# Per-head sums of a delta-rule layer, taken transposed and spread back by a sixteen-row product

## The reference, cut to what matters

```
xs_j = x + mu_j * (x_before - x)                # six mixes of a token and the one before it
r, k, v = xs_0 W_r, xs_1 W_k, xs_2 W_v          # three 1024x1024 products
decay, a = two low-rank products (rank 64) of xs_3, xs_4
g  = sigmoid(xs_5 G1) G2                        # the gate, a low-rank product (rank 128)
kk = k * k_k / max(|k * k_k| over a head, 1e-12)    # sum "kk"
bonus = (sum over a head of r * k * r_k) * v        # sum "bonus"
y  = delta rule(r, decay, k, v, kk, a)
y  = (y - mean over a head) / sqrt(variance over a head + 64e-5)   # sums "mean", "var"
out = ((y * gn_g + bonus + gn_b) * g) W_o
```

## Time and profile before

| | us |
|---|---|
| median of 3 runs | 2188.06 (2187.59 to 2189.05) |
| the profiled execution, its own time | 2188.55 |
| its span, first to last instruction | 2186.7 |
| TensorE busy | 2125.8 (97%) |
| VectorE busy | 1523.9 (70%) |
| ScalarE busy | 1171.2 (54%) |
| GpSimd busy | 380.8 (17%) |
| mean granted TensorE clock | 0.994 of full speed |

### The profile page before, as it was taken

One profiled execution on the slowest core, in us unless ns is written; L12 is line 12 of the kernel. 1 busy time (PEld: TensorE's weight loads), 2 busy tenths in 40 slices (PEclk: granted clock), 3 DMA queues, 4 the chain that ended last, 5 costly groups with the idle time before them and its releaser, 6 DMA issues.

```text
span 2186.7 us, 40730 instructions
## 1 busy us (share of the span) xinstructions
PE 2125.8 (97%) x16760; PEld 1912.0 (87%) x16760; DVE 1523.9 (70%) x2118; ACT 1171.2 (54%) x2038; POOL 380.8 (17%) x357
## 2 busy tenths in 40 slices
PE   8999999999999999999999999999999988999998
PEld 5888989888888889889888998988889978898887
DVE  6797757688769877676876686477567544647754
ACT  4564456565546644675655575465447532446542
POOL 0141022111102110221111003120142540123001
PEclk9999999999999999999999999999999999999999
DMA  7987772467768877625666555355543400434552
GB/s 303 356 301 271 263 251 98 164 238 265 247 235 294 295 251 275 228 88 174 214 219 205 185 173 177 111 176 183 192 147 123 154 4 3 144 122 164 186 188 98
DMA packets 116680, 424.61 MB, mean 194 GB/s; under 512 B 12944, under 2 KB 14736, under 8 KB 115600
## 3 DMA queue, kind: packets, MB, share of 16 engines
q1 hardware_dynamic: 112896, 409.52, 53.6%
q10 hardware_dynamic: 3600, 12.49, 1.5%
HBM read 418.29 MB, written 3.67 MB: 193 GB/s over the span
## 4 chain that ended last, share of the span: by engine, by line
PE 84%; DVE 6%; issue 4%; ACT 4%; POOL 1%; DMA 1%; SPq 0%; DVEq 0%; ACTq 0%; POOLq 0%
PE banks L598 82%; DVE weight_lower L1715 2%; POOL heap L3018 1%; PE banks L1132 1%; ACT weight_upper L2444 1%; DMA weight_ring<-w_ada_row_dram 0%; PE banks L1535 0%; DVE heap L2209 0%; ACT xn_t L2622 0%; DVE xn_t L1936 0%; DMA weight_ring<-w_in_dram 0%; DVE heap L2055 0%; DVE xn_t L1933 0%; ACT heap L2655 0%; DVE silu L1930 0%
## 5 line engine op out<-in xcount | busy, mean ns | idle before, releaser
L1715 DVE TENSOR_TENSOR weight_lower<-weight_ring,weight_upper 128x1024 fp32r<-128x1024 f32 x580 | 742.2, 1287 | 278.0 <-ACT weight_upper L2444 276.5
L598 PE MATMUL banks<-xn_halves,weight_upper 128*128 128x512 f32 (+1 forms) x3680 | 809.6, 342 | 0.8 <-DVE xn_halves L2038 0.7
L2444 ACT ACTIVATE weight_upper<-weight_ring 128x1024 fp32r<-128x1024 f32 x580 | 607.9, 1054 | 283.6 <-PE banks L598 189.7
L598 PEld LDWEIGHTS banks<-xn_halves,weight_upper 128*128 128x128 f32 x3680 | 619.2, 190 | 63.5 <-issue 1.1
L598 PE MATMUL banks<-xn_halves,weight_lower 128*128 128x256 f32 x2832 | 525.9, 284 | 4.5 <-DVE xn_halves L1748 2.1
L598 PEld LDWEIGHTS banks<-xn_halves,weight_lower 128*128 128x128 f32 x2832 | 436.7, 191 | 29.1 <-DVE xn_halves L1748 3.2
L598 PE MATMUL banks<-hidden,weight_upper 128*128 128x512 f32 x1216 | 312.0, 395 | 0.6 <-DVE heap L2180 0.6
L3018 POOL TENSOR_TENSOR heap<-heap 128x256 f32<-128x256 f32 x120 | 121.9, 1020 | 884.9 <-ACT heap L2741 590.5
L598 PEld LDWEIGHTS banks<-hidden,weight_upper 128*128 128x128 f32 x1216 | 215.6, 188 | 40.0 <-DVE heap L2180 0.7
L1726 DVE CUSTOM_DVE_ANT_0 weight_ring<-weight_ring,c_rows,vecs 128x1024 f32<-128x1024 f32 x140 | 185.8, 1331 | 20.9 <-DMA weight_ring<-w_ada_dram 20.4
L598 PEld LDWEIGHTS banks<-hidden,weight_lower 128*128 128x128 f32 x1216 | 166.7, 188 | 16.2
(11 more groups left out here) (312 smaller groups left out, 2402.8 us busy)
## 6 DMA issues: line engine op xcount, KB each, us to landing
weight_ring<-w_ada_dram SPq DMA_DIRECT2D x140, 512.0 KB, 4.6
weight_ring<-ffn_gate_dram SPq DMA_DIRECT2D x88, 512.0 KB, 3.8
weight_ring<-ffn_up_dram SPq DMA_DIRECT2D x88, 512.0 KB, 4.5
weight_ring<-ffn_down_dram SPq DMA_DIRECT2D x88, 512.0 KB, 3.4
weight_ring<-m_w_up_dram SPq DMA_DIRECT2D x64, 512.0 KB, 3.2
weight_ring<-m_w_down_dram SPq DMA_DIRECT2D x64, 512.0 KB, 3.2
weight_ring<-w_in_dram SPq DMA_DIRECT2D x58, 512.0 KB, 3.9
weight_ring<-b_w_rkv_dram SPq DMA_DIRECT2D x24, 512.0 KB, 3.8
```

The costliest lines, as they stand in the source:

```text
L598: return nc.tensor.matmul(o, w, r, start=first, stop=last)
L1715: V.tensor_tensor(w_lo[:, n % RING, :], ring[:, n % RING, :], w_hi[:, j % SPLITS, :].bitcast(F32), ALU.subtract).then_inc(*did("weight_low ...
L2444: A.activation(w_hi[:, j % SPLITS, :], ring[:, n % RING, :], ACT.Copy).then_inc(*did("weight_upper", j))
```

## The change

Four things change, all in this layer.

1. **Head sums transposed.** `head_of` becomes a 128x32 matrix of zeros with two columns of ones in it. For block k a window of 16 columns is taken from it, so that the ones stand in columns 2k and 2k+1; it is the stationary operand, and the data, 128x256, is the moving one. Eight products accumulate into 16 partitions of bank 6: heads on partitions, tokens along the row.
2. **Spread by a sixteen-row product.** A new constant `of_head`, 16 rows by 1024 columns, has a one where a head owns a channel. Block k is the product of its 16x128 piece (stationary) with the 16x256 numbers (moving). The four `widen` copies go, and the steps between sum and spread work on 16x256 numbers instead of 128x32.
3. **Gate input by one VectorE operation.** `xs_5` is made like `xs_0` to `xs_2`; ScalarE's eight parts go, and VectorE makes the eight blocks of `xs_5` in one go after those of `xs_0`.
4. **The gate's low-rank product later.** `lora_in(5)` moves behind item 2 of the r projection, and ScalarE's sigmoid with it.

`head_of` and `of_head` lie in `delta_consts`, which grows from 128x832 to 128x1888 numbers in one transfer; TensorE waits for it before `head_sums("kk")`.

```diff
-    c["head_of"] = np.kron(np.eye(2), np.ones((RN, 1)))
+    at = np.arange(2 * RH)[None, :]
+    c["head_of"] = at == RH - 1 + np.arange(P)[:, None] // RN
+    c["of_head"] = np.zeros((P, D))
+    c["of_head"][0:RH] = np.kron(np.eye(RH), np.ones((1, RN)))
...
-        wide = {n: slots(i, QT * RH * RN) for n, i in (("kk", 5), ("bonus", 11), ("mean", 4), ("var", 5))}
+        per_head = {n: slots(i, S)[0:RH, :] for n, i in (("kk", 5), ("bonus", 11), ("mean", 4), ("var", 5))}
...
-                    for t in range(QT):
-                        mn = mm(bank[:, 6, t * RH + 2 * k:t * RH + 2 * k + 2],
-                                src[:, k, t * P:(t + 1) * P], const("head_of"), True, True)
+                    a = RH - 1 - 2 * k
+                    mn = mm(bank[0:RH, 6, 0:S], const("head_of")[:, a:a + RH], src[:, k, :], k == 0, k == KD - 1)
...
-                    for t in range(QT):
-                        c = t * RH + 2 * k
-                        mn = mm(cols(b, P, (k % 2) * S + t * P), wide[name][:, c * RN:(c + 2) * RN], ident,
-                                True, True)
+                    mn = mm(cols(b, S, (k % 2) * S), const("of_head", RH)[:, k * P:(k + 1) * P], per_head[name],
+                            True, True)
...
-                lora_in(5, P)
+                pe.wait_ge(*of("delta_consts_in", 0))
                 head_sums("kk", kk_sq, "kk_sq")
...
                     if f in (1, 3):
                         lora_pair(2 * f - 2)
+                    if f == 2:
+                        lora_in(5, P)
...
-                shifted_halves(0, 5)
+                shifted_halves(0)
+                for k in range(KD):
+                    dve.wait_ge(*due("xs_lower", (1, k)))
+                    shifted(5, k)
                 dve.wait_ge(*due("rkv_raw", (1, KD - 1)))
                 shifted_halves(2)
...
-                step(V.tensor_scalar(stat[:, 0, :], stat[:, 0, :], 1e-12, None, ALU.max))
-                step(V.reciprocal(stat[:, 0, :], stat[:, 0, :]))
-                widen("kk", 0)
+                step(V.tensor_scalar(kk, kk, 1e-12, None, ALU.max))
+                step(V.reciprocal(kk, kk), [("head_stat", "kk")])
...
-                    act.wait_ge(*due("xs_lower", (1, f)))
-                    part(5, f)
                     xs_upper(0, f)
                 for k in range(KD):
                     xs_upper(2, k)
                 act.wait_ge(*due("head_sums", "kk"))
-                A.activation(stat[:, 0, :], bank[:, 6, 0:QT * RH], ACT.Sqrt).then_inc(
+                A.activation(per_head["kk"], bank[0:RH, 6, 0:S], ACT.Sqrt).then_inc(
-                lora(5, P, ACT.Sigmoid)
...
                     if f in (1, 3):
                         lora_pair(2 * f - 2)
+                    if f == 2:
+                        lora(5, P, ACT.Sigmoid)
```

More of the change, by code:

```diff
@@ L118 @@
 ATTN = [k for k in CONSTS if k == "turn" or k.startswith(("causal", "alibi", "cmp"))]
-DELTA = ["before", "upto", "eye", "levels", "within"]
+DELTA = ["before", "upto", "eye", "levels", "within", "head_of", "of_head"]
 CONST_AT, CONST_W = packed([(k, v.shape[1]) for k, v in CONSTS.items() if k not in ATTN + DELTA])
@@ L285, in program @@
         den = sb("den", [P, 4, HPG])
-        stat = sb("stat", [P, 4, QT * RH])
+        sb("stat", [P, 4, QT * RH])
         w_end = sb("w_end", [P, KD, NCH])
@@ L2196, in pair @@
                 return slice(2 * b, 2 * b + 2), bank[:, b, :].rearrange("p (k t) -> p k t", k=2)
-            def widen(name, m):
-                w = wide[name].rearrange("p (h n) -> p h n", n=RN)
-                step(V.tensor_copy(w, bcast(stat[:, m, :], RN)), [("head_stat", name)])
             MU = {0: 0, 1: 2, 2: 3, 3: 1, 4: 4, 5: 5}
@@ L2206, in shifted @@
                 mu, x = vec("mu", MU[j] * KD + k), xs_t[j][:, k, :]
-                if j >= 3:
+                if j in (3, 4):
                     dve.wait_ge(*due("xs_part", (j, k)))
@@ L2214, in shifted, with shifted_halves @@
                         *did("xs", (j, k)))
-            def shifted_halves(j, other=None):
+            def shifted_halves(j):
                 for k in range(KD):
                     shifted(j, k)
-                    if other:
-                        shifted(other, k)
                     for done in [k - 1] * (k > 0) + [k] * (k == KD - 1):
@@ L2238, in delta_mixer @@
                 dve.wait_ge(*due("head_root", "kk"))
-                step(V.tensor_scalar(stat[:, 0, :], stat[:, 0, :], 1e-12, None, ALU.max))
-                step(V.reciprocal(stat[:, 0, :], stat[:, 0, :]))
-                widen("kk", 0)
+                kk = per_head["kk"]
+                step(V.tensor_scalar(kk, kk, 1e-12, None, ALU.max))
+                step(V.reciprocal(kk, kk), [("head_stat", "kk")])
                 dve.wait_ge(*due("delta_consts_in", 0))
@@ L2269, in delta_mixer @@
                 dve.wait_ge(*due("head_sums", "bonus"))
-                step(V.tensor_copy(stat[:, 1, :], bank[:, 6, 0:QT * RH]), [("head_sums_read", "bonus")])
-                widen("bonus", 1)
+                step(V.tensor_copy(per_head["bonus"], bank[0:RH, 6, 0:S]),
+                     [("head_stat", "bonus"), ("head_sums_read", "bonus")])
                 for b in range(4):
@@ L2287, in delta_mixer @@
                 dve.wait_ge(*due("head_sums", "mean"))
-                step(V.tensor_scalar(stat[:, 2, :], bank[:, 6, 0:QT * RH], 1.0 / RN, None, ALU.mult),
-                     [("head_sums_read", "mean")])
-                widen("mean", 2)
+                step(V.tensor_scalar(per_head["mean"], bank[0:RH, 6, 0:S], 1.0 / RN, None, ALU.mult),
+                     [("head_stat", "mean"), ("head_sums_read", "mean")])
                 used("mean", 2, xn, xn, ALU.subtract)
                 dve.wait_ge(*due("head_sums", "var"))
-                step(V.tensor_scalar(stat[:, 3, :], bank[:, 6, 0:QT * RH], 1.0 / RN, GN_EPS, ALU.mult, ALU.add),
+                var = per_head["var"]
+                step(V.tensor_scalar(var, bank[0:RH, 6, 0:S], 1.0 / RN, GN_EPS, ALU.mult, ALU.add),
                      [("head_var", 0), ("head_sums_read", "var")])
                 dve.wait_ge(*due("head_root", "var"))
-                step(V.reciprocal(stat[:, 3, :], stat[:, 3, :]))
-                widen("var", 3)
+                step(V.reciprocal(var, var), [("head_stat", "var")])
                 used("var", 3, xn, xn, ALU.mult)
@@ L2917, in delta_mixer @@
                 act.wait_ge(*due("head_var", 0))
-                A.activation(stat[:, 3, :], stat[:, 3, :], ACT.Sqrt).then_inc(*did("head_root", "var"))
+                A.activation(per_head["var"], per_head["var"], ACT.Sqrt).then_inc(*did("head_root", "var"))
                 for k in range(KD):
```

## The result

The change made the kernel slower where a gain of 0.3% was forecast.

| | before | after |
|---|---|---|
| median of 20 runs, us | 2190.72 | 2196.52 |
| profiled execution, its own time, us | 2188.55 | 2197.34 |
| its span, us | 2186.7 | 2195.5 |
| TensorE, VectorE, ScalarE busy, us | 2125.8, 1523.9, 1171.2 | 2132.0, 1519.1, 1166.8 |
| mean granted TensorE clock | 0.994 | 0.989 |

A forecast was written before the change was run, and what follows sets the result against it. TensorE, busy 97% of the span, was taken to bound the kernel. Gains 4.3 - 0.9 - 0.2 + 2.7 + 0.6 = 6.5 us took 2188.55 to 2182.05, less 0.49 for the median: 2181.5 us; 8-in-10 range 2177.5 to 2186.3.

The forecast's parts named there:

- part 2: Spreads of kk and bonus: each 3.67 us before and 3.74 after, a loss of 0.2 us together.
- a rival with a narrow operand and a falling clock: Bonus and mean sums: the clock falls all the same, gain only 2.4 us, time 2185.6 us; chance 0.13.
- part 4: Mean and variance sums and spreads, with the steps between: a gain of 0.6 us in all.
- What the clock took: Behind the new idle stretch ahead of the first lora_pair: a clock loss of 0.9 us, bounds 0 and 5.2.
- part 1: The kk sums and the moved gate product, up to the second pair: 4.3 us gained, less 0.9 for the clock.
- My row against it: An earlier idle stretch of 2.20 us with clock 1.00 around it, set against the rule that idle gaps lower the clock.
- The idling: Ahead of the first lora_pair: TensorE idles 2.9 us waiting for ScalarE's root of the kk sums, bounds 1.5 and 4.
- Part 1's gain: At the second pair: start at 1687.2 against 1691.51, 4.3 us gained, less 0.9 for the clock.
- Part 3: Bonus sums and the item behind them: 6.61 us with no clock fall, a gain of 2.7 us.
- Prices of narrow tiles: Each new sum or spread of eight products: 3.74 us including 0.30 for tile changes, bounds 3.44 and 4.0.

The follow-up runs named there:

- e6: Against e5, only the spread's two operands changed, to 16 rows instead of 128; median 2187.67 us, ratio to before 0.9986.
- e5: The changed kernel with the full-row operands of e1 and the early square root of e2 together; median 2178.51 us, ratio to before 0.9943.
- e3: The changed kernel with the two gate edits undone, leaving transposed sums and sixteen-row spreads; median 2191.40 us, ratio to before 1.0004.
- e1: The changed kernel with sums' window 128 columns wide and spreads over 128 rows, filled with zeros; median 2184.97 us, ratio to before 0.9976.
- e8: The changed kernel with lora_in(5) behind item 1 of the r projection, ahead of the first pair; median 2189.25 us, ratio to before 0.9994.
- e2: The changed kernel with ScalarE's kk square root ahead of the upper halves of xs_2; median 2186.89 us, ratio to before 0.9981.
- e7: Against e5, bonus and mean are summed and spread in one product with a 128x128 block of ones; median 2171.76 us, ratio to before 0.9910.
- e9: Against e5, only the spread's operands changed, to 64 rows instead of 128; median 2180.62 us, ratio to before 0.9954.
- e4: The kernel before with only the gate's two edits (xs_5 by VectorE, lora_in(5) later); median 2191.64 us, ratio to before 1.0003.

## Why the prediction was wrong

- **The step that failed, part 2: each spread was booked at 0.1 us more, the difference of 3.74 and 3.67, and the clock behind it at nothing.** The 3.72 us of the spread itself are right where no fall lies in it (kk, variance; with one the row reads 4.9). The price stands mostly behind it, in products that the change doesn't touch: the step at kk cost 1.8 us, at bonus 3.2, behind the variance 1.9, and mean and variance came out 3.0 worse than part 4 had it. e6 against e5 gives the four together as 9.2 us. I had a rival with a narrow operand and a falling clock, chance 0.13, but priced it at the sums, took away gains with it and added no loss. At sums with 16 columns and all 128 rows no fall began, but for the one in e3 behind 1.92 us of idling.
- **What the clock took in part 1: I took 0.9 us.** It was 2.8 (6.03 us at 0.53). Ahead of the first pair both traces with over 4 us of idling (after, e1) show the fall, those with 1.06 and none (e8, e2) don't. The rule that I had weighed and set aside, the Trainium skill, "TensorE: Matmul & The Clock Gate", "Why this matters for your kernels", that idle gaps bring the clock down, agrees with the trace. My row against it, 2.20 us of idling and no fall, was the luck of one execution: the same stretch stands in the delta core of all twelve kernels, and in ten, all but before and after, a fall begins in it or within 1.3 us behind. e6:

```profile
1836.41 4.57 PE L601 MATMUL banks<-heap 64*64 64x64 f32 x159 [2.20 <-DVE spare L2394]
...
1837.00:1838.00 1.00, 1.00 (x50) 1.00 (x45) 0.00 (x0) 0.00 (x0) 0.00 (x0) 0.50 0.00 0
```

  Small products stand around it, so it does not show that 2.20 us of idling are enough.
- **The idling: 4.41 instead of 2.9 us, just outside its bounds (1.5 to 4).** TensorE was ready at 1674.56, less 1.54 that is 1673.0, as forecast (1673.1). ScalarE's root ended 1.1 us later than forecast, and the pair began another 0.3 behind it. VectorE's run of blocks of xs_5 started late, since a weight cut of 1.2 us stands before the last lower half of xs_0, which I had left out. VectorE and ScalarE, after:

```profile
1666.03 1.21 DVE L1717 TENSOR_TENSOR weight_lower<-weight_ring,weight_upper 128x1024 fp32r<-128x1024 f32 x1
1667.16 0.83 DVE L1750 TENSOR_TENSOR shifted_lower<-heap,shifted_upper 128x256 fp32r<-128x256 f32 x1
1667.91 4.03 DVE L2211 SCALAR_TENSOR_TENSOR heap<-heap,vecs,xn_t 128x256 f32<-128x256 f32 x10
...
1676.98 1.28 ACT L2878 ACT_TABLE_LOAD   x1
1678.28 0.37 ACT L2878 ACTIVATE heap<-banks 16x256 f32<-16x256 f32 x1
```

- **Part 1's gain: 4.3 less 0.9 forecast, 0.2 measured.** The mechanism was right, with `lora_in(5)` at 3.62 us on the path; the idling and the clock ate it.
- **Part 3: right.** 3.55 + 3.14 = 6.69 us against 6.61 forecast, clock 1.00.
- **Part 4: right but for the clock.** From the end of the variance sums to the spread 2.87 us against 2.95, a wait of 0.44 us. The reciprocal, after:

```profile
L2295 DVE RECIPROCAL heap<-heap 16x256 f32<-16x256 f32 x1 | 1.7, 1742 | 0.5 <-ACT heap L2915 0.5
```

- **Prices of narrow tiles: right, a little high.** From the start of a block to the next product 3.55 us for the kk sums (1665.13 to 1668.68) and 3.64 for the kk spread (1700.56:1704.20), against 3.74.
- **Not settled.** 0.7 us in the delta core: the clock is low for 6.8 us there after and for 3.4 before, and this differs from profile to profile (3.4 in e5 and e7, 10.2 in e2), among small products that the change doesn't touch.

Put together: forecast -6.5 for the layer, measured +7.3. The misses by the table of marks: 3.2 up to the second pair, 1.7 at the kk spread, 0.2 at bonus's sums, 3.1 at its spread, 0.7 in the core, 3.0 at mean and variance, 1.9 behind them: 13.8, the whole difference. In absolute time the forecast was 2181.5 and the measurement 2196.52, 15.0 apart: 12.3 of that is the change by its medians (5.8 slower, 6.5 faster forecast), and 2.7 the base, whose first three runs had their median at 2188.06 and all twenty at 2190.72.

## What to carry to other kernels

Price a small product by what it does to the clock behind it as well as by its own records: here four blocks of 3.7 us with 16 rows cost 9.2 us more, most of it in the work that follows, and filling the operands with zeros up to 64 or 128 rows gave this back. When an edit lets TensorE arrive earlier, follow the next wait on each engine's queue and look for work, or a reordering, that fills or removes it; an idle stretch of 4.41 us cost another 2.8 behind it. Where a sum is only spread back, a block of ones does both in one product. And look at more than one execution before a single row counts as proof that the clock holds.

## What was unexpected of the hardware

- The clock fell during or at most 0.9 us behind 18 of 20 blocks of 16 back-to-back products with 16 rows and 256 columns, TensorE being busy throughout. The Trainium skill, "Perfetto Trace Analysis", "Matmul Optimizations", says that TensorE scales power by utilization and asks for products back to back in batches. Here they were back to back (3.64 busy of 3.64 us at 1700.56), and the clock fell to 0.50 all the same: on this row the rule is not enough, the rows in use count.
- Rows of zeros kept the clock up like rows of numbers (e1, e5, e9).
- Sums with two moving columns and full rows do the same as few rows: in before a fall begins at two of the four (bonus, mean), in e4 at all four.
- The VectorE reciprocal takes 1.74 us for 256 columns both on 16 partitions (after) and on 128 (1.75 in e5).
